# The second half of the first feed-forward layer computed by quarter products, in a two-block transformer kernel on one Trainium2 core

## What is computed

```
cond = silu(c)
for i in range(2):
    mod = (cond @ ada_w[i] + ada_b[i]).reshape(1, 3, 3, 1024)
    h = adaln(x, norm_g[i, 0], mod[:, 0, 0], mod[:, 0, 1])
    x = x + 0.5 * (1 + mod[:, 0, 2]) * swiglu(h, ffn_w_in[i, 0], ffn_w_out[i, 0])
    h = adaln(x, norm_g[i, 1], mod[:, 1, 0], mod[:, 1, 1])
    x = x + (1 + mod[:, 1, 2]) * (pool_mixer if i == 0 else fox_attention)(h, ...)
    h = adaln(x, norm_g[i, 2], mod[:, 2, 0], mod[:, 2, 1])
    x = x + 0.5 * (1 + mod[:, 2, 2]) * swiglu(h, ffn_w_in[i, 1], ffn_w_out[i, 1])

def swiglu(h, w_in, w_out):          # w_in 1024 x 5632, w_out 2816 x 1024
    g, u = jnp.split(h @ w_in, 2, axis=-1)
    return (jax.nn.silu(g) * u) @ w_out
```

## Time and profile before

| | |
|---|---|
| median of three runs | 2896.26 us (2895.88 to 2897.73) |
| the profiled execution | 2896.0 us, its span 2893.6 us |
| TensorE busy | 2873.8 us, 99% of the span |
| VectorE busy | 1939.4 us, 67% |
| ScalarE busy | 1264.7 us, 44% |
| DMA | 366.99 MB moved, mean 127 GB/s |

### The profile page before, as it was taken

How to read it: one execution, slowest core, us unless ns; L and a number is a source line. 1 busy time by engine, 2 the same in 40 slices (tenths; PEclk the granted TensorE clock), 3 DMA queues, 4 the chain that set the end, 5 groups by cost and what they waited for, 6 DMA issues and landing times. The chain is left out here.

```text
span 2893.6 us, 40922 instructions
## 1 busy us (share of the span) xinstructions
PE 2873.8 (99%) x16099; PEld 2485.7 (86%) x16099; DVE 1939.4 (67%) x2624; ACT 1264.7 (44%) x1752; POOL 144.9 (5%) x297
## 2 busy tenths in 40 slices
PE   8999999999999999999999999999999999999999
PEld 7888889899898998868999988788888888888887
DVE  8667688777786777876856758766535467754453
ACT  4223255344452445474533445654414348443332
POOL 0111100100001001040000000200000001000000
PEclk9999999999999999999999999999999999999999
DMA  7867613524236243251332322413232222232231
GB/s 299 272 217 255 210 45 115 206 109 154 89 115 230 91 168 107 88 182 61 108 126 79 114 91 88 160 63 110 87 105 98 95 81 95 96 108 95 88 109 66
DMA packets 100944, 366.99 MB, mean 127 GB/s; under 512 B 11248, under 2 KB 11808, under 8 KB 100784
## 3 DMA queue, kind: packets, MB, share of 16 engines
q1 hardware_dynamic: 77616, 276.56, 27.9%
q0 software_dynamic: 23168, 88.17, 8.8%
HBM read 362.51 MB, written 2.18 MB: 126 GB/s over the span
## 5 line engine op out<-in xcount | busy, mean ns | idle before, releaser
L1263 DVE TENSOR_TENSOR wl<-raw,wh 128x1024 fp32r<-128x1024 f32 x393 | 477.1, 1226 | 519.4 <-ACT wh L697 518.9
L697 ACT ACTIVATE wh<-raw 128x1024 fp32r<-128x1024 f32 x393 | 409.8, 1054 | 752.4 <-PE PS L2131 685.1
L2131 PE MATMUL PS<-HH,wh 128*128 128x512 f32 x1560 | 608.2, 390 | 0.4 <-DVE HL L1979 0.3
L2131 PE MATMUL PS<-HL,wh 128*128 128x512 f32 x1560 | 607.7, 390 | 0.0
L2131 PE MATMUL PS<-HH,wl 128*128 128x512 f32 x1560 | 607.7, 390 | 0.0
L2131 PEld LDWEIGHTS PS<-HH,wh 128*128 128x128 f32 x1560 | 293.1, 188 | 62.1 <-DVE HL L1979 0.8
L2131 PEld LDWEIGHTS PS<-HH,wl 128*128 128x128 f32 x1560 | 293.0, 188 | 60.5
L2131 PEld LDWEIGHTS PS<-HL,wh 128*128 128x128 f32 x1560 | 293.1, 188 | 60.3
L2131 PE MATMUL PS<-AH,wh 128*128 128x512 f32 x848 | 330.7, 390 | 0.5 <-DVEq L2014 0.5
L2131 PE MATMUL PS<-AL,wh 128*128 128x512 f32 x848 | 330.5, 390 | 0.0
L2131 PE MATMUL PS<-AH,wl 128*128 128x512 f32 x848 | 330.3, 390 | 0.0
(11 more groups left out here) (346 smaller groups left out, 5107.6 us busy)
## 6 DMA issues: line engine op xcount, KB each, us to landing
raw<-in_stream SPq DMA_DIRECT2D x459, 512.0 KB, 3.4
acc<-in_stream POOLq DMA_DIRECT2D x54, 512.0 KB, 4.9
WK<-in_stream SPq DMA_DIRECT2D x42, 512.0 KB, 4.5
piece<-in_stream POOLq DMA_DIRECT2D x38, 512.0 KB, 5.0
WK<-in_stream POOLq DMA_DIRECT2D x24, 512.0 KB, 6.6
arena<-in_stream SPq DMA_DIRECT2D x16, 512.0 KB, 12.5
HT<-in_stream POOLq DMA_DIRECT2D x12, 512.0 KB, 6.8
TBa<-negcum POOLq DMA_DIRECT2D x8, 640.0 KB, 5.0
```

The lines of the kernel that those rows point to most:

```text
L697: F(wh[:, r, :], raw[:, r, :], ACT.Copy).then_inc(hi_done, 1)
L1263: TT(wl[:, r, :], raw[:, r, :], wh[:, r, :].bitcast(F32), ALU.subtract).then_inc(lo_done, 1)
L2131: mm = MM(PS[g % 2][:, j, :], l, x, start=(first and i == 0), stop=(last and i == 2), skip_group_check=after_halves)
```

## The change

FFN 1 gets quarter products for all five groups of its second half (`FAST[0] = (0, 5)`), with its 20 chunks of weights packed as 20 quarters. Three more things are changed.

- The four input sums are made on VectorE among the plain groups 3 to 5 of the first half, and their high and low parts (four ScalarE copies, four VectorE subtractions) right behind the sixth. TH lies over the tiles `acc[:, 0]`, TL over `acc[:, 1]`. The copy of cond therefore moves from `acc` to the tile `bands` at the start, goes to `acc` at the end of FFN 1 and back to `bands` at FFN 2; the table that used to be in `bands` is loaded later.
- The modulation sums are dealt out anew: in FFN 1 60 in place of 80 (30 among the plain groups over six buffers, 20 in the output stage of the first half, three behind each split, and 10 in that of the second), in FFN 2 and FFN 3 34 each (24 in the first output stage, three behind each split, and 10 in the second). In a first output stage the last six sums have two buffers, `piece` and `HT`, since the two in `WK` take the first quarters, whose load now waits only for the last sum in WK and not for all.
- `late_constants` moves behind the first output group of FFN 1.

The core of the diff:

```diff
-FAST = {2: (4, 5), 3: (4, 5), 5: (4, 5)}
-ADA_BY = {0: 8 + 3 * NADA, 2: 8 + 4 * NADA, 3: 8 + 5 * NADA}
-ADA_EARLY = ADA_BY[0]
-ADA_PHASES = (16, 8)
+FAST = {0: (0, 5), 2: (4, 5), 3: (4, 5), 5: (4, 5)}
+ADA_EARLY = 30
+ADA_PHASES = {0: (20, 10), 2: (24, 10), 3: (24, 10)}
+ADA_BY = {0: 60, 2: 94, 3: 128}
+ADA_PLACE = [2, 3, 0] + [4, 5, 6]
+def late_places():
+    places = []
+    for into_part, behind in ADA_PHASES.values():
+        places += [(0, 1, 2, 3)[i % 4] if i < into_part - 6 else i % 2 for i in range(into_part)]
+        places += [(0, 1, 2, 3)[i % 4] for i in range(behind)]
+    return places
+ADA_PLACES = [ADA_PLACE[m % len(ADA_PLACE)] for m in range(ADA_EARLY)] + late_places()
+def ada_free(m):
+    earlier = [i for i in range(m) if ADA_PLACES[i] == ADA_PLACES[m]]
+    return max(earlier[-1] + 1, ADA_EARLY if m >= ADA_EARLY else 0) if earlier else 0
...
-        ada_late = [piece[:, 0:1024], HT[:, :, :].rearrange("p a t -> p (a t)"),
-                    *(WK[:, 2 * i:2 * i + 2, :].rearrange("p k t -> p (k t)") for i in range(2))]
-        ada_tiles = [acc[:, 1, 1024:2048], acc[:, 1, 2048:3072], piece[:, 0:1024]]
+        ada_tiles = [piece[:, 0:1024], HT[:, :, :].rearrange("p a t -> p (a t)"),
+                    *(WK[:, 2 * i:2 * i + 2, :].rearrange("p k t -> p (k t)") for i in range(2)),
+                     *(acc[:, 0, 1024 * i:1024 * i + 1024] for i in range(3))]
... (GpSimd)
+                    if part:
+                        pl.wait_ge(a_ready, part["e"] + part["n"] + 1)
+                    else:
+                        pl.wait_ge(mix_ready, 4)
                     for i in range(n):
-                        pl.wait_ge(ada_step, max(m - 3, ADA_EARLY))
+                        load_ada(m)
... (ScalarE, first half of FFN 1)
+                            act.wait_ge(ada_step, ADA_EARLY)
+                            for i in range(4):
+                                mix_high(i, st["sets"])
...
+                                if st is plan[2] and half == 0 and c + nt != c_last:
+                                    late_constants()
... (VectorE, first half of FFN 1)
                             for u in range(2, ng):
                                 for i in range(4):
                                     split_until(c + RING + 1 + i)
-                                    n = (2 if i < 3 else 1) if st is plan[2] else 1 if i < 3 else 2
-                                    ada_until(min(ada, at["ada"] + n))
+                                    ada_until(ADA_EARLY if u == 5 and i == 3 else at["ada"] + (1 if u < 5 and i == 3 else 2))
+                                    if (u, i) == (2, 1):
+                                        whole(0, 0, 0, sets)
...
                                 hidden_group(st, e, g, cv, j, 2 * u, 0)
-                            if paired:
-                                late_constants()
+                            for i in range(4):
+                                mix_low(i, sets)
... (VectorE, output groups)
-                                splits_with_sums(c + nt // 2 + RING, 2 if st["parts"] else 1, ada or at["ada"])
-                                if half == 1 and st["parts"]:
-                                    fast_groups(st, st["parts"][1],
+                                ahead = c + nt != c_last and st["at"][1]
+                                splits_with_sums(c + nt // 2 + RING, 3 if ahead else 2,
+                                                 0 if ada is None else ada - ADA_PHASES[st["gate"]][1] if ahead else ada)
+                                if half == 1 and ahead:
+                                    fast_groups(st, ahead,
                                                 lambda: add_out(st, g, c + nt // 2, 4, gate))
                                 else:
                                     add_out(st, g, c + nt // 2, 4 * half, gate)
+                                if st is plan[2] and half == 0 and ahead:
+                                    late_constants()
```

More of the change, by code:

```diff
@@ L59 @@
 NADA = 24
-ADA_RING = 3
 FAST_SLOTS = 6
@@ L170, in make_plan @@
         elif kind == "ffn":
-            st["parts"], st["sets"] = [], sum(bool(p.get("parts")) for p in plan[:-1])
+            st["parts"], st["at"], st["sets"] = [], [None, None], sum(bool(p.get("parts")) for p in plan[:-1])
             for half, (ng, nt) in enumerate(f["halves"]):
@@ L179, in make_plan @@
                                             s=at["fs"] + add["fs"], f=at["fg"] + add["fg"], turn=-7 * nf % RING, slot=(8 - 4 * nf) % FAST_SLOTS,
-                                            tile=2 * (ng - nf), sums=ADA_BY[f["gate"]] - ADA_PHASES[1] if late else 0))
+                                            tile=2 * (ng - nf), sums=max(m + 1 for m in range(ADA_BY[f["gate"]] - ADA_PHASES[f["gate"]][1])
+                                                      if ADA_PLACES[m] in (2, 3)) if late else 0))
+                    st["at"][half] = st["parts"][-1]
                 add["fs"] += 7 * nf
@@ L1329, in add_out, with ada_sum @@
                     ins.then_inc(x_ready if t < 3 else bank_free, 1)
[L1331 to L1333 removed]
+            def ada_sum(tile, s, j):
+                return nc.vector.tensor_tensor_reduce(tile, tile, condc, 1.0, 0.0, ALU.mult, ALU.add, mod[:, s, j:j + 1])
             def ada0(m):
@@ L1801, in _ @@
-                        if ada and not st["parts"]:
-                            paired = st is plan[2] and c == st["c"]
-                            if paired:
-                                split_until(c + 10)
-                                hidden_group(st, e, g, cv, j, 0, 0)
-                                split_until(c + 11)
-                                hidden_group(st, e + 1, g + 1, cv + 1, j + 1, 2, 0)
-                                split_until(c + 12)
-                                e, cv, g, c, j = e + 2, cv + 2, g + 2, c + 8, j + 2
-                            for u in range(2 if paired else 0, ng):
+                                fast_groups(st, part, None)
@@ new lines, in _ @@
+                            e, cv, g, c, j, ng = e + ng, cv + ng, g + ng, part["c"], j + ng, 0
+                        elif st is plan[2]:
+                            split_until(c + 10)
+                            hidden_group(st, e, g, cv, j, 0, 0)
+                            split_until(c + 11)
+                            hidden_group(st, e + 1, g + 1, cv + 1, j + 1, 2, 0)
+                            split_until(c + 12)
+                            e, cv, g, c, j = e + 2, cv + 2, g + 2, c + 8, j + 2
+                            for u in range(2, ng):
@@ L1828, in _ @@
                         e, cv, g, c, j = e + 2 * pairs, cv + 2 * pairs, g + 2 * pairs, c + 8 * pairs, j + 2 * pairs
-                        if ng % 2 and not ada and not st["parts"]:
+                        if ng % 2 and not part:
                             split_until(c + 4 + RING)
@@ L2541, in _ @@
                                 group(c, g, nt, a_tile, (lambda k: [(a_ready, e + k // 2 + 2)]),
-                                      begun=1 if half == 0 and st["parts"] else 0)
+                                      begun=1 if half == 0 and part else 0)
                             c, g = c + nt // 2, g + 1
```

145 lines of the change are left out of this document (81 added, 64 removed).

## The result

| | before | after |
|---|---|---|
| median | 2896.38 us (2895.88 to 2897.73) | 2924.03 us (2921.84 to 2925.32) |
| profiled execution, its span | 2896.0, 2893.6 us | 2925.3, 2923.2 us |
| granted clock, mean | 0.999 | 0.995 |

The ratio is 1.0094, with a 95% interval of 1.0076 to 1.0111. The kernel is slower by 27.7 us; the forecast was 2911.0, the range 2895 to 2922. The direction was right; the time lies 2 us above the range, and the loss is nearly twice the 14.7 of the sum.

What follows compares the result with a forecast made beforehand. The prediction took TensorE, busy 2873.8 of 2893.6 us, as the bound. Its terms, -8.0 + 13 + 1.7 + 2 x 4 = +14.7 us on 2896.0, gave 2911 us, range 2895 to 2922.

Steps and rivals of the forecast that it cites:

- The quarter products' 8.0 us: FFN 1's second half: five plain groups of 108.8 us become 35 products of 2.88 us, 100.8 us, saving 8.0 us.
- rival 4: The skill's isolated matmul spacing holds: TensorE saves 11.9 us in place of 8.0, on top of the waits; 2907 us, chance 0.03.
- FFN 1's wait of 13 us: FFN 1's first output stage: VectorE splits chunk 34 at 216 to 217, so TensorE waits 13 us, some 2 before chunk 33.
- One clock fall of 1.7 us: Behind FFN 1's wait: TensorE's clock falls once, at mean 0.57 over 4 us, costing 1.7 us; ends 0 and twice that.
- 4 us each in FFN 2 and 3: First output stage's 24 sums delay the third product's low part; TensorE waits 4 us in each FFN, ends 0 and 7.
- rival 3: Slower still: clock falls in all three FFNs and first quarters' loads delay the sums; +28 us, 2924 us, chance 0.07.
- Rivals 1 and 2: 1: only FFN 1 waits, 2898 to 2903 us, chance 0.20. 2: sums never make VectorE late, 2888 us, chance 0.13.
- (a): Sign in FFN 1's second half: matmuls of 256 columns at 0.120 us, 100.8 us in all.
- (b): Sign in FFN 1: TensorE idle some 11 us before chunk 34, ended by VectorE's split; VectorE waiting for `piece` and `HT`.
- (d): Sign in FFN 1: a second low-clock stretch near 217 us.
- (c): Sign in FFN 1's tail: GpSimd's loads issued by turns, each 0.3 us behind a sum, landing in 5 to 6 us.
- (e): Sign in FFN 2 and 3: TensorE idle 3 to 5 us at the third product of the second quarter part.

Runs made afterwards that it cites:

- v_seven: Changed kernel with six buffers for sums, last six over four, FFN 1's first three loads early, small constants ahead of its second half's first output group: 2889.1 us.
- e_deal: Changed kernel with FFN 2 and 3 given back the earlier 16 and 8 sums, last 20 modulation sums left out (timing only): 2903.9 us.
- e_start: Changed kernel with FFN 1's first three output-stage loads issued before the wait for low parts, and another buffer order in all three FFNs: 2916.9 us.
- e_hold: Changed kernel with the first quarters' loads waiting for all sums of the output stage; the tail keeps two buffers: 2921.3 us.
- e_tail4: Changed kernel with the last six sums over four buffers (`piece`, `HT`, idle tiles `PR` and `SG`), quarters' loads still early: 2902.4 us.
- e_const: Changed kernel with only the small constants moved, behind the first output group of FFN 1's second half: 2921.1 us.
- e_front: Changed kernel with only the small constants moved, ahead of the first output group of FFN 1's first half: 2920.3 us.
- e_four: Changed kernel with all first-output-stage sums over the same four buffers to the end (`piece`, `HT`, two in `WK`): 2909.6 us.

## Why the prediction was wrong in size

- **The quarter products' 8.0 us: right.** v_seven's FFN 1 gains 7.96 us with no wait in it. The 11.9 of the isolated spacing (rival 4) is excluded by the same number; the spacing stays 0.120 us, as in the earlier trace rows.
- **FFN 1's wait of 13 us: right, a little small.** 14.3 measured (12.3 in e_deal), the split of chunk 34 at 216.6 where 216 to 217 was given, the first wait ahead of chunk 33 at 3.8 and not 2. Its parts were named rightly: late start (6.4 in e_start, with the reordered loads in it), small constants (about 5), two-buffer tail with the burst in front of it (2.6 to 4.6 of it the burst's, in e_hold). They overlap, since each takes away from the same two waits. The steps came at their times (the 14th sum ended at 193.3, the 18th at 209.2), but in part by luck. The stage's first two waits for loads were 3.0 and 1.2 us, not 4.4 and 1.8. And the equal landings of 5.3 to 6.0 us were not what happened: two took 7.1 and 6.9, those behind them 3.9 and 4.9. The mean, 5.7, was right, the pattern was not.
- **One clock fall of 1.7 us: mis-sized and miscounted, half of the miss.** In the changed kernel's trace the losses are 28.7, 14.0 more than the sum's 14.7: 1.3 is FFN 1's wait, 0.8 and 4.3 are the waits of FFN 2 and 3, and 7.4 is the clock. The one in FFN 1 cost 3.0, since the low clock lasted through 5.7 us of work. Three more followed in FFN 2 and 3 (6.1 us together). I took the size from the pool mixer's 4 us row and asked only of the 11 us wait whether it would bring a fall.
- **4 us each in FFN 2 and 3: the term that failed.** Measured 7.7 and 11.6, outside the ends 0 to 7. FFN 2's waits alone, 4.8, lie in the 3 to 5 that were given; what failed there is the clock, for which the sum has no term in FFN 2 and 3 and gives no reason: the fall cost 2.8 us. In FFN 3 the waits are 8.3, and the clock adds 3.3. The steps of the wait were wrong in two places. "With the round trips above" put the 18th sum's end at 579 and the 24th's at 599 to 601; less the 9.5 us by which the trace of after is late at that stage's start, they ended at 581.4 and 603.1 in FFN 2, and later still in FFN 3. The tail's first landing behind the burst took 8.0 us (the load of `piece` issued at 589.48, its sum at 597.45), not 5.3 to 6.0. And the chain was followed to the third product alone: the first low part stands right behind the 24th sum, so that already the given 599 to 601 put its end at 600.2 to 602.2, for a product wanted at 600.7. So in place of one wait at the third product there were two and more, ahead of the first product too. What the tail needed is shown by e_tail4: the same burst, two more buffers, and FFN 2's 7.7 us are gone. The cause stood in the change as it was read: the quarters' loads now wait only for the last sum in `WK`, so they start in the tail, and I used them for the upper end alone.
- **The rivals.** What happened is rival 3, which had a chance of 0.07: clock falls in all three FFNs, tails slowed by the first quarters' loads, 2924. The range was cut at 2922 against it. That its sum is met to the microsecond is luck: its parts were 17, 5.1 and 14, and 14.3, 9.1 and 13.1 were measured. It should have had more, because the parts are not independent: the burst stands ahead of the tail in all three FFNs, and most waits of 3 us or more cost clock. Rivals 1 and 2 needed landings near 4 and 3 us. e_hold shows 3.5, and even then FFN 1 waits 9.7 us. By an estimate from that, half a microsecond less for each of the tail's three round trips would take off 1.5, so rival 2's condition would not have been enough; no run shows it.
- **Signs to look for.** (a), (b) and (d) came as written; of (c) the turns of the loads but not their landing; of (e) the wait at the third product in FFN 3 (3.2 us), while FFN 2 had 1.2 there and 3.3 ahead of the first. FFN 3 loses 4 us more than FFN 2 with the same code; e_tail4 shows the same order (0.0 and 3.8). The traces show one difference ahead of the burst: the stage's first load takes 7.4 us to land in FFN 3 and 4.9 in FFN 2 (8.0 and 4.4 in e_tail4), and the 18th sum starts 1.7 us later (2.8 in e_tail4). It is not the whole: in e_hold, with 4.3 and 4.7 us, FFN 3 still loses 1.6 more. Why that load is slower, and what the rest is, stays open.

## What to carry to other kernels

Where buffers are few, what counts is the slowest round trip and not the mean one: look for the burst of other loads that the change puts right in front of it. When a change gives a faster engine part its buffers early, the work that shared them needs as many others; here two idle tiles brought the change from 28 us slower to 6 (e_tail4), and with earlier first loads and the constants moved as well it is 7 us faster. And on a TensorE that is otherwise never idle, add a fall of the clock to the price of a wait of 3 us or more: 24 of the 28 such waits had one here, at 1.6 to 3.0 us for each of the four in the changed kernel.

## What the runs showed of the hardware

Not every wait brought TensorE's clock to the lower level. Over the traces of the changed kernel and of the experiments on it, in FFN 1 to 3, all ten waits of 4.0 us and more have such a fall in them or right behind them (up to 1.4 us), and so have 14 of the 18 waits of 3.0 to 3.8 us. Those without one are the 3.8 us in the changed kernel's FFN 1, and one of 3.0 to 3.2 each in e_const, e_front and e_tail4. Of the six from 2.3 to 2.8 us two have one (e_hold and e_const in FFN 3, each some 7 us behind another wait with a fall), of the five from 1.1 to 1.6 none.

In e_four a wait of 3.2 us in FFN 2 (3.06 in the profile's bracket) is followed by 0.50 for 4 us; in e_tail4 one of the same length in FFN 3 keeps the full clock. Their stretches, e_four's first:

```profile
608.00:612.00 4.00, 1.08 (x10) 0.94 0.01 2
612.00:616.00 4.00, 3.86 (x18) 0.50 0.00 0
616.00:620.00 4.00, 4.00 (x27) 0.71 0.72 261
```

```profile
956.00:960.00 4.00, 1.50 (x13) 1.00 0.01 2
960.00:964.00 4.00, 3.44 (x29) 1.00 0.02 4
964.00:968.00 4.00, 4.00 (x36) 1.00 0.74 255
```

With waits of equal length the one FFN loses 6.4 us and the other 3.8, and that difference is the lower clock, 2.8 us in e_four. The Trainium skill's rule named above fits most of these places; it does not tell the four that kept the full clock from the others.

A 512 KB load of GpSimd's took 3.3 to 3.8 us to land where little else moved (e_hold's tail in FFN 1, behind its first two), and 7 to 8 with three or four loads of SyncE's issued just ahead of it.
